# Hybrid decoder layer with hierarchical MoE, one core: TensorE's combination and gather spread between weight halves, parts of h and of the output made one pair later

## The chip, the cores and the metric

The kernel runs on one core of a Trainium2 chip. The metric is the device time of one execution in microseconds; three executions of the kernel before gave a median of 925.91 us (925.41 to 926.84).

## The reference

One decoder layer over 256 tokens of width 1024. First a mixing sub-layer: one projection of the normed input into a short gated convolution, a GLU with a 31-tap convolution and a cross-attention, merged by gates and projected again. Then the part that this case is about, the mixture of experts:

```python
g_sel = argmax(softmax(z @ w_group + b_group))          # 1 of 4 groups
top2  = top_k(softmax(e_logits of that group), 2)       # 2 of its 8 experts
for e in range(32):
    gate, up = split(z @ w_gate_up[e], 2)               # 1024 -> 2 x 512
    y += combine[:, e] * ((silu(gate) * up) @ w_down[e])   # 512 -> 1024
out = rms_norm(x + y, final_norm_g)
```

All arithmetic is float32 in the reference. The 32 experts' weights are 201 MB, and all of them are read.

## The kernel before

**Split weights.** TensorE multiplies with operands of the rounded type fp32r, so each float32 weight is used as a sum of two parts. A weight "half" is a tile of 128 x 2048 float32. It arrives in `raw` by DMA (two halves a transfer, six slots); ScalarE (ACT) makes the rounded part `hi` (`expert_hi`, L578), VectorE (DVE) makes `lo = raw - hi` (`expert_lo`, L932), and TensorE (PE) multiplies both. The `hi` and `lo` rings hold four halves (three and `hi_last`/`lo_last`): `expert_hi` of half N waits until TensorE has used half N-4. SyncE (SP) issues the next transfer into a raw slot once both `lo` parts of the slot are made (`lo_made`).

**Pairs.** Experts e and e+16 make a pair; there are 16 pairs, numbered i from 0. A pair has eight halves for gate and up and four for down. All experts' tokens of a pair are put into 2 x 64 slots by one-hot matmuls. A `step(j, r)` on each engine handles pair i = 2j + r: steps (0,0) and (0,1) are written out, the other 14 are in a hardware loop. Down halves of a pair are used in the next pair's step. In a step, halves have numbers k: 0 to 3 are gate (into PSUM bank G0), 4 to 7 up (G1), 8 to 11 the downs of pair i-1 (banks DN, the same two banks 6 and 7 that the gather writes). Halves 12 and 13 are halves 0 and 1 of the next step.

**The small work of a pair**, beside the halves:
- TensorE: `gather` (48 bf16 matmuls, L1305) picks the next pair's tokens out of `z_parts` into banks 6 and 7; `picked` (8 small ones, L1382 and L1387) makes the slots' weights and the transposed one-hot matrix in G0 and signals `slotted`; the fold matmuls (L1397, L1407) turn gate and up; `combine` (8 matmuls, L1341) adds the output of pair i-2 to the sums in banks 0 to 3.
- ScalarE: `gate_out` (`gu_sb`, L637) copies G0 out, `expert_xeT` (L484) makes the rounded part of the gathered tokens, `put` (L647) copies the transposed one-hot matrix out of G0, `up_out` (L654), `silu_sb` (L660), `hT_hi` (L616) rounds h, `y_out` (`y_hi`, L611) rounds the output in DN.
- VectorE: `xeT_lo` (L997), `slot_weights` (`fold2` L1048 and `comb_slot` L1051), `make_pick` (L1004), h = silu x up (L1083, `h_made`), `hT_lo` (L1041), `y_out_lo` (two instructions, L1055).

**Order.** Each engine runs its list in the order written, and semaphores join them. `put` waits for `comb_slot_made` as well as for `slotted`, since it and DVE's `slot_weights` read the same bank G0:

```python
expert_xeT(i + 1, (r + 1) % 2)
more(8)
act.wait_ge(comb_slot_made, i + 1)
act.wait_ge(slotted, i + 1)
nc.scalar.activation(put[:, r, :], G0[:, T:2 * T], ACT.Copy).then_inc(put_made, 1)
more(9)
```

`more(k)` is half k's `expert_hi` on ScalarE and `expert_lo` on VectorE. In the steps but the first the order of ScalarE is halves 2, 3, 4, 5, `gate_out`, 6, 7, `expert_xeT`, 8, `put`, 9, 10, `up_out`, 11, silu, 12, 13, `hT_hi`, `y_out`; that of VectorE is halves 2 to 7, `xeT_lo`, `slot_weights`, 8, 9, `make_pick`, 10, 11, 12, h, 13, `hT_lo`, `y_out_lo`; that of TensorE is halves 0, 1, `combine`, 2, 3, `gather`, 4, 5, `picked`, 6, 7, fold of gate, 8, 9, fold of up, 10, 11. In the first step there are no downs, and halves 0 to 3 are made ahead of it.

Of the kernel before, what the change touches and what calls it, by code (L numbers as in the profile page):

```python
# [23 lines left out]
KT = D // P  # L24
TT = T // P
# [13 lines left out]
STEP = 12  # L39
# [36 lines left out]
DENSE = 2 * N_UNITS  # L76
# [16 lines left out]
def hybrid_moe_kernel(nc, x, mem, w_dense, w_experts, w_route, cols, rows, consts, out):  # L93
    ctx = ExitStack()
    with ctx:
# [91 lines left out]
        hi_made, lo_made, half_used = sem("hi_made"), sem("lo_made"), sem("half_used")  # L187
# [35 lines left out]
        G0, G1 = ps[:, 4, :], ps[:, 5, :]  # L223
# [163 lines left out]
        def _(act):  # L387
# [93 lines left out]
            def expert_xeT(i, par):  # L481

                act.wait_ge(gathered, i + 1)
                nc.scalar.activation(xeT[:, par, :, :, 0:SLOTS], gathered_view(), ACT.Copy).then_inc(xeT_hi, 1)  # L484
# [120 lines left out]
            nc.scalar.activation(ident_bf[:, :], ident, ACT.Copy).then_inc(ident_made, 1)  # L605
            expert_xeT(0, 0)

            def y_out(i, used):

                act.wait_ge(half_used, used)  # L610
                nc.scalar.activation(y_hi[:, :], ps[:, 6:8, :].rearrange("p a b -> p (a b)"), ACT.Copy).then_inc(y_hi_made, 1)  # L611

            def hT_hi(i):

                act.wait_ge(h_made, i + 1)
                nc.scalar.activation(hT[:, :, :, 0:SLOTS], h_sb[:, :, :, :], ACT.Copy).then_inc(h_hi, 1)  # L616

            def step(j, r):


                start = isinstance(j, int) and j == 0 and r == 0
                i = 2 * j + r
                at_half = 0 if start else STEP * r - 4
                used = 2 * STEP * j + (DENSE + at_half)

                def more(*halves):
                    for k in halves:
                        expert_hi(j, at_half, k)

                if start:  # L630
                    more(4, 5)
                else:
                    more(2, 3, 4, 5)
                act.wait_ge(half_used, used + 4)
                if not start:
                    act.wait_ge(gate_folded, i)
                nc.scalar.activation(gu_sb[:, 0:FF], G0, ACT.Copy).then_inc(gate_out, 1)  # L637
                more(6, 7)
                if start:
                    act.wait_ge(comb_made, 1)  # L640
                    act.wait_ge(loops_made, 1)
                expert_xeT(i + 1, (r + 1) % 2)
                more(8)

                act.wait_ge(comb_slot_made, i + 1)
                act.wait_ge(slotted, i + 1)
                nc.scalar.activation(put[:, r, :], G0[:, T:2 * T], ACT.Copy).then_inc(put_made, 1)  # L647
                more(9)
                if not start:
                    more(10)  # L650
                act.wait_ge(half_used, used + 8)
                if not start:
                    act.wait_ge(up_folded, i)
                nc.scalar.activation(gu_sb[:, FF:2 * FF], G1, ACT.Copy, scale=comb_slot[:, r:r + 1]).then_inc(up_out, 1)  # L654
                if not start:
                    more(11)
                act.wait_ge(gate_folded, i + 1)
                if not start:
                    act.wait_ge(h_lo, i)
                nc.scalar.activation(silu_sb[:, :, :, :].rearrange("p f x s -> p (f x s)"), G0, ACT.Silu).then_inc(silu_made, 1)  # L660
                if not start:
                    more(12, 13)
                    act.wait_ge(half_used, used + 12)
                hT_hi(i)
                if not start:
                    y_out(i - 1, used + 12)

            step(0, 0)
            step(0, 1)
# [2 lines left out]
            with act.Fori(1, last_turn + 1) as j:  # L672
                step(j, 0)
                step(j, 1)
            expert_hi(last_turn, 2 * STEP - 4, 2)
            expert_hi(last_turn, 2 * STEP - 4, 3)
            act.wait_ge(half_used, 2 * STEP * last_turn + (DENSE + 2 * STEP))
# [15 lines left out]
        def _(dve):  # L693
# [340 lines left out]
                link(nc.vector.tensor_tensor(stat[:, 13:14], stat[:, 13:14], stat[:, 14:15], ALU.add))  # L1034
            nc.vector.tensor_scalar(loops[:, 0:1], stat[:, 13:14], float(TURNS - 1), None, ALU.add).then_inc(loops_made, 1)

            def hT_lo(i):

                dve.wait_ge(h_made, i + 1)
                dve.wait_ge(h_hi, i + 1)  # L1040
                nc.vector.tensor_tensor(hT[:, :, :, SLOTS:2 * SLOTS], h_sb[:, :, :, :], hT[:, :, :, 0:SLOTS].bitcast(f32),  # L1041
                                        ALU.subtract).then_inc(h_lo, 1)

# [14 lines left out]
            def step(j, r):  # L1058
                first = isinstance(j, int)
                i = 2 * j + r  # L1060
                start = first and i == 0
                at_half = 0 if start else STEP * r - 4

                def more(*halves):
                    for k in halves:
                        expert_lo(j, at_half, k)

                if start:
                    more(4, 5, 6, 7)
                else:  # L1070
                    more(2, 3, 4, 5, 6, 7)
                xeT_lo(i + 1, (r + 1) % 2)
                slot_weights(i, r)
                more(8, 9)
                make_pick(r, slice(r + 2, r + 3) if first else bass.ds(2 * j + (r + 2), 1))
                if not start:
                    more(10, 11, 12)
                dve.wait_ge(silu_made, i + 1)
                dve.wait_ge(up_folded, i + 1)
                if not start:  # L1080
                    dve.wait_ge(h_lo, i)
                up = G1[:, 0:4 * SLOTS].rearrange("p (f o s) -> p f o s", o=1, s=SLOTS).to_broadcast([P, 4, 2, SLOTS])
                nc.vector.tensor_tensor(h_sb[:, :, :, :], silu_sb[:, :, :, :], up, ALU.mult).then_inc(h_made, 1)  # L1083
                if not start:
                    more(13)
                hT_lo(i)
                if not start:
                    dve.wait_ge(y_hi_made, i)
                    for g in range(2):
                        y_out_lo(g, DN[g], y_lo_made)  # L1090

            step(0, 0)
            step(0, 1)
# [2 lines left out]
            with dve.Fori(1, last_turn + 1) as j:  # L1096
                step(j, 0)
                step(j, 1)
            expert_lo(last_turn, 2 * STEP - 4, 2)
            expert_lo(last_turn, 2 * STEP - 4, 3)  # L1100
            dve.wait_ge(half_used, 2 * STEP * last_turn + (DENSE + 2 * STEP))
            for g in range(2):
# [13 lines left out]
        def _(pe):  # L1116
# [176 lines left out]
            mm(ps[:, 5, 2 * PAIRS:3 * PAIRS], ones, either[:, 1, :], start=False, stop=True).then_inc(ranked, 1)  # L1293


            def gather(i, par):

                pe.wait_ge(pick_made, i + 1)
                for c in range(KT):
                    dst = ps[:, 6 + c // 4, c % 4 * 2 * SLOTS:(c % 4 + 1) * 2 * SLOTS]  # L1300
                    for k in range(3 * TT):
                        part_, t = k // TT, k % TT
                        if isinstance(i, int) and i == 0 and c == 0:
                            pe.wait_ge((z_part0, z_part1, z_part2)[part_], t + 1)
                        last = mm(dst, z_parts[:, part_, t, c * P:(c + 1) * P],  # L1305
                                  pick2[:, par, t, 0:2 * SLOTS],
                                  start=(k == 0), stop=(k == 3 * TT - 1))
                last.then_inc(gathered, 1)

            def gate_or_up(j, at_half, k, par):  # L1310

# [21 lines left out]
                                      stop=(x == 1 and h == 1 and kt == 1 and w is lo), skip_group_check=True)  # L1333
                last.then_inc(half_used, 1)

            def combine(par):

                for t in range(TT):
                    for g in range(2):
                        for y in (y_hi[:, g * 512:(g + 1) * 512], y_lo[g][:, :]):  # L1340
                            last = mm(Y[2 * t + g], put[:, par, t * P:(t + 1) * P], y,  # L1341
                                      start=False, stop=False, skip_group_check=True)
                    last.then_inc(combined, 1)
# [5 lines left out]
            def step(j, r, q):  # L1349
# [9 lines left out]
                if not first:  # L1359
                    pe.wait_ge(put_made, i - 1)  # L1360
                    pe.wait_ge(y_lo_made, 2 * i - 2)
                    combine(r)
                gate_or_up(j, at_half, 2, r)
                gate_or_up(j, at_half, 3, r)
                gather(i + 1, (r + 1) % 2)
                if not start:
                    pe.wait_ge(h_made, i)
                else:
                    pe.wait_ge(loops_made, 1)
                gate_or_up(j, at_half, 4, r)  # L1370
                gate_or_up(j, at_half, 5, r)

                pe.wait_ge(gate_out, i + 1)
                def picked(t, x):
# [42 lines left out]
            with pe.Fori(1, last_turn + 1) as j:  # L1417
                step(j, 0, bass.ds(j % TURNS * 2, 1))
                step(j, 1, bass.ds(j % TURNS * 2 + 1, 1))

            pe.wait_ge(put_made, 2 * last_turn + 1)
            pe.wait_ge(y_lo_made, 4 * last_turn + 2)
            combine(0)
            pe.wait_ge(silu_made, 2 * last_turn + 2)
            pe.wait_ge(h_made, 2 * last_turn + 2)
            pe.wait_ge(h_lo, 2 * last_turn + 2)
            for k in range(4):
                down(last_turn, 2 * STEP - 4, k, k // 2, (G0, G1))
            pe.wait_ge(put_made, 2 * last_turn + 2)
            pe.wait_ge(last_lo, 2)  # L1430
            combine(1)
# [54 lines left out]
```

## Time and profile before

| | |
|---|---|
| median of 3 executions | 925.91 us |
| the profiled execution's own time | 929.3 us |
| its span (first to last instruction) | 927.5 us |
| PE / DVE / ACT busy in the span | 873.3 / 814.4 / 621.7 us |
| expert stage, first to last h (L1083) | 432.3 to 898.9 us |

The profile is one execution. Its instructions have start times from the beginning of the span. A row of the timeline gives start, duration, engine, line, operation, tiles and count, and in brackets how long the engine sat idle before it and what ended that. An instruction's duration on ScalarE, VectorE and TensorE reaches a little beyond the start of the next one, since they are pipelined, so the time that an instruction takes from its engine's list is the distance between two starts.

### The profile page before, as it was taken

To read this page: it belongs to the slowest core of one execution; us is meant where nothing else is said; L and a number is where in the kernel's file an instruction comes from. 1 tells how busy PE (TensorE), PEld (TensorE's weight loads), DVE (VectorE), ACT (ScalarE), POOL (GpSimd) and SP (SyncE) were. 2 spreads that over 40 slices of the span, in tenths; PEclk is the share of its full clock that TensorE was granted. 3 is DMA by queue.
4 is the path that set the end of the run, shared out by engine and by line. 5 is a ranking of instruction groups with operands and counts; after the bars stand their busy time and mean duration, and the time that the engine had idled before them with its cause. 6 is when DMAs were issued, how large, how long until landed. Compare 5 with 4: busy or idle time off the path is not lost.

```text
span 927.5 us, 14508 instructions
## 1 busy us (share of the span) xinstructions
PE 873.3 (94%) x5734; PEld 751.2 (81%) x5734; DVE 814.4 (88%) x818; ACT 621.7 (67%) x537; POOL 11.0 (1%) x19
## 2 busy tenths in 40 slices
PE   5999999999999899868999999999999999999975
PEld 5999999999899899657877777777777877777764
DVE  5358999999867957488999999999999999999993
ACT  5563434345453573558888878888888878887882
POOL 0110000000000000020000000000000000000000
PEclk9999999999999999979999999999999999999997
DMA  9952545455443486518999999999999999999911
GB/s 379 374 183 97 210 155 194 170 184 194 159 155 119 182 317 267 211 37 327 384 400 399 411 395 407 398 411 400 401 408 408 396 400 406 409 398 396 423 66 45
DMA packets 20146, 270.64 MB, mean 292 GB/s; under 512 B 2192, under 2 KB 2448, under 8 KB 3856
## 3 DMA queue, kind: packets, MB, share of 16 engines
q1 hardware_dynamic: 19696, 268.59, 73.0%
q10 hardware_dynamic: 416, 1.57, 0.5%
q8 instruction: 24, 0.39, 0.2%
q14 instruction: 10, 0.08, 0.0%
HBM read 269.10 MB, written 1.05 MB: 291 GB/s over the span
## 4 chain that ended last, share of the span: by engine, by line
PE 48%; DVE 30%; issue 14%; ACT 6%; DMA 1%; DVEq 1%; SPq 0%; ACTq 0%
DVE lo L932 10%; PE ps L1317 10%; PE ps L1146 9%; PE ps L1147 9%; PE ps L1148 9%; DVE lo_last L932 7%; ACT hi L578 5%; PE ps L1305 3%; DVE lo L704 2%; DVE conv L791 2%; PE ps L1161 2%; PE ps L1163 2%; PE ps L1162 2%; DVE y_lo L1055 1%; DVE hT L1041 1%
## 5 line engine op out<-in xcount | busy, mean ns | idle before, releaser
L932 DVE TENSOR_TENSOR lo<-raw,hi 128x2048 fp32r<-128x2048 f32 x142 | 323.5, 2287 | 7.6 <-ACT hi L578 6.6
L578 ACT ACTIVATE hi<-raw 128x2048 fp32r<-128x2048 f32 x141 | 264.2, 1909 | 3.5 <-PE ps L1317 3.5
L1317 PE MATMUL ps<-hi,xeT 128*128 128x512 f32 x384 | 158.4, 412 | 15.1 <-DVE lo L932 11.2
L704 DVE TENSOR_TENSOR lo<-raw,hi 128x2048 fp32r<-128x2048 f32 x62 | 141.7, 2288 | 30.0 <-ACT hi L396 28.5
L1146 PE MATMUL ps<-inA,hi 128*128 128x256 f32 x576 | 165.1, 287 | 1.6 <-DVE lo L704 1.1
L1147 PE MATMUL ps<-inA,hi 128*128 128x256 f32 x576 | 163.8, 284 | 0.0
L1148 PE MATMUL ps<-inA,lo 128*128 128x256 f32 x576 | 163.7, 284 | 0.0
L396 ACT ACTIVATE hi<-raw 128x2048 fp32r<-128x2048 f32 x63 | 120.6, 1914 | 63.6 <-PE ps L1148 41.0
L1317 PE MATMUL ps<-lo,xeT 128*128 128x512 f32 x384 | 150.7, 392 | 0.0
L1146 PEld LDWEIGHTS ps<-inA,hi 128*128 128x128 f32 x576 | 111.4, 193 | 2.7 <-DVE lo L704 2.6
L1147 PEld LDWEIGHTS ps<-inA,hi 128*128 128x128 f32 x576 | 111.5, 194 | 0.1
L1148 PEld LDWEIGHTS ps<-inA,lo 128*128 128x128 f32 x576 | 111.4, 193 | 0.0
L1317 PEld LDWEIGHTS ps<-hi,xeT 128*128 128x128 f32 x384 | 72.1, 188 | 47.9 <-DVE lo L932 31.2
L932 DVE TENSOR_TENSOR lo_last<-raw,hi_last 128x2048 fp32r<-128x2048 f32 x48 | 109.7, 2285 | 0.0
L791 DVE SCALAR_TENSOR_TENSOR conv<-u_sb,col,conv 128x255 f32<-128x255 f32 (+29 forms) x240 | 94.1, 464 | 0.0
L578 ACT ACTIVATE hi_last<-raw 128x2048 fp32r<-128x2048 f32 x48 | 91.6, 1909 | 0.0
L1317 PEld LDWEIGHTS ps<-lo,xeT 128*128 128x128 f32 x384 | 72.2, 188 | 13.2
L1146 PE MATMUL ps<-inB,hi 128*128 128x256 f32 x256 | 72.7, 284 | 0.9 <-DVE lo L704 0.9
L1147 PE MATMUL ps<-inB,hi 128*128 128x256 f32 x256 | 72.4, 283 | 0.0
L1148 PE MATMUL ps<-inB,lo 128*128 128x256 f32 x256 | 72.4, 283 | 0.0
L1331 PE MATMUL ps<-hi,hT 128*128 128x512 f32 x192 | 63.9, 414 | 0.0
L1331 PE MATMUL ps<-lo,hT 128*128 128x512 f32 x192 | 60.2, 395 | 0.0
(214 smaller groups left out, 1229.5 us busy)
## 6 DMA issues: line engine op xcount, KB each, us to landing
raw<-in_w_experts SPq DMA_DIRECT2D x96, 2048.0 KB, 9.8
raw<-in_w_dense SPq DMA_DIRECT2D x29, 2048.0 KB, 7.8
raw<-in_w_dense SPq DMA_DIRECT2D x2, 1024.0 KB, 8.1
x_sb<-in_x SPq DMA_DIRECT2D x1, 1024.0 KB, 4.8
mem_sb<-in_mem SPq DMA_DIRECT2D x1, 1024.0 KB, 15.5
x_again<-in_x ACTq DMA_DIRECT2D x1, 1024.0 KB, 5.0
out<-x SPq DMA_DIRECT2D x2, 512.0 KB, 2.7
ffn_row<-in_rows ACTq DMA_DIRECT2D x1, 512.0 KB, 7.4
```

Source lines behind the costliest of these rows:

```text
L396: return nc.scalar.activation(conv_half(hi, N), raw_half(slot, h), ACT.Copy)
L578: nc.scalar.activation(expert_half(hi, N0), raw_flat(slot, k % 2), ACT.Copy).then_inc(hi_made, 1)
L704: nc.vector.tensor_tensor(conv_half(lo, N), raw_half(slot, h), conv_half(hi, N).bitcast(f32), ALU.subtract).then_inc(lo_made, 1)
L791: nc.vector.scalar_tensor_tensor(conv[:, c, shift:T], u_sb[:, c, 0:T - shift], w, conv[:, c, shift:T], ALU.mult, ALU.add).then_inc(conv_st ...
L932: nc.vector.tensor_tensor(expert_half(lo, N0), raw_flat(expert_slot(m), k % 2), expert_half(hi, N0).bitcast(f32), ALU.subtract).then_inc(l ...
L1146: mm(dst, w_hi[:, k, c * P:(c + 1) * P], acts[:, 0, k, :], start=(k == 0), stop=False)
L1147: mm(dst, w_hi[:, k, c * P:(c + 1) * P], acts[:, 1, k, :], start=False, stop=False)
L1148: last = mm(dst, w_lo[:, k, c * P:(c + 1) * P], acts[:, 0, k, :], start=False, stop=(k == KT - 1))
L1161: mm(dst, acts[:, 0, 4 * h + k, tok], w_hi[:, k, :], start=first, stop=False, skip_group_check=True)
L1305: last = mm(dst, z_parts[:, part_, t, c * P:(c + 1) * P], pick2[:, par, t, 0:2 * SLOTS], start=(k == 0), stop=(k == 3 * TT - 1))
L1317: last = mm(dst, xeT[:, par, 4 * (k % 2) + kt, k // 2 % 2, :], expert_half(w, N)[:, kt * 512:(kt + 1) * 512], start=(k % 4 == 0 and kt == ...
L1331: last = mm(DN[g], hT[:, 2 * h + kt, x, :], expert_half(w, N)[:, a:a + 512], start=(x == 0 and h == 0 and kt == 0 and w is hi), stop=(x == ...
```

## The change

The combination of pair i-2 is cut in two (token tile 0 before half 2, tile 1 before half 3) and the gather in three (three, three and two column tiles, after halves 3, 4 and 5; its start flags now stand once per bank). `hT_hi`, `hT_lo` and `y_out`, `y_out_lo` move from the end of a step into the next step. ScalarE makes half 6 before `gate_out`, and halves 7 and 8 after it; VectorE makes half 8 before `xeT_lo`. After the last step, the last pair's first three down halves go before `combine(0)`. The core of the diff (ScalarE, VectorE, TensorE in turn):

```diff
                 if start:
-                    more(4, 5)
+                    more(4, 5, 6)
                 else:
-                    more(2, 3, 4, 5)
+                    more(2)
+                    if not isinstance(j, int):
+                        y_out(used)
+                    more(3, 4)
+                    act.wait_ge(half_used, used)
+                    hT_hi(i)
+                    more(5, 6)
                 act.wait_ge(half_used, used + 4)
...
-                more(6, 7)
                 if start:
+                    more(7)
                     act.wait_ge(comb_made, 1)
                     act.wait_ge(loops_made, 1)
+                else:
+                    more(7, 8)
                 expert_xeT(i + 1, (r + 1) % 2)
-                more(8)
-
                 act.wait_ge(comb_slot_made, i + 1)
                 act.wait_ge(slotted, i + 1)
                 nc.scalar.activation(put[:, r, :], G0[:, T:2 * T], ACT.Copy).then_inc(put_made, 1)
+                if start:
+                    more(8)
                 more(9)
...
                 if not start:
                     more(12, 13)
-                    act.wait_ge(half_used, used + 12)
-                hT_hi(i)
-                if not start:
-                    y_out(i - 1, used + 12)
...
+            act.wait_ge(half_used, 2 * STEP * last_turn + (DENSE + 2 * STEP - 4))
+            hT_hi(2 * last_turn + 2)
+            y_out(2 * STEP * last_turn + (DENSE + 2 * STEP - 4))
             expert_hi(last_turn, 2 * STEP - 4, 2)
             expert_hi(last_turn, 2 * STEP - 4, 3)
```
```diff
-                    more(2, 3, 4, 5, 6, 7)
+                    more(2)
+                    if not first:
+                        dve.wait_ge(y_hi_made, i - 1)
+                        for g in range(2):
+                            y_out_lo(g, DN[g], y_lo_made)
+                    more(3, 4)
+                    hT_lo(i)
+                    more(5, 6, 7, 8)
                 xeT_lo(i + 1, (r + 1) % 2)
                 slot_weights(i, r)
-                more(8, 9)
+                if start:
+                    more(8)
+                more(9)
                 make_pick(r, slice(r + 2, r + 3) if first else bass.ds(2 * j + (r + 2), 1))
...
                     more(13)
-                hT_lo(i)
-                if not start:
-                    dve.wait_ge(y_hi_made, i)
-                    for g in range(2):
-                        y_out_lo(g, DN[g], y_lo_made)
...
+            hT_lo(2 * last_turn + 2)
             expert_lo(last_turn, 2 * STEP - 4, 2)
+            dve.wait_ge(y_hi_made, 2 * last_turn + 1)
+            for g in range(2):
+                y_out_lo(g, DN[g], y_lo_made)
             expert_lo(last_turn, 2 * STEP - 4, 3)
```
```diff
-                    combine(r)
+                    combine(r, (0,))
                 gate_or_up(j, at_half, 2, r)
+                if not first:
+                    combine(r, (1,))
                 gate_or_up(j, at_half, 3, r)
-                gather(i + 1, (r + 1) % 2)
+                gather(i + 1, (r + 1) % 2, (0, 1, 2))
...
                 gate_or_up(j, at_half, 4, r)
+                gather(i + 1, (r + 1) % 2, (3, 4, 5))
                 gate_or_up(j, at_half, 5, r)
+                gather(i + 1, (r + 1) % 2, (6, 7))
...
-            pe.wait_ge(put_made, 2 * last_turn + 1)
-            pe.wait_ge(y_lo_made, 4 * last_turn + 2)
-            combine(0)
             pe.wait_ge(silu_made, 2 * last_turn + 2)
             pe.wait_ge(h_made, 2 * last_turn + 2)
             pe.wait_ge(h_lo, 2 * last_turn + 2)
-            for k in range(4):
-                down(last_turn, 2 * STEP - 4, k, k // 2, (G0, G1))
+            down(last_turn, 2 * STEP - 4, 0, 0, (G0, G1))
+            down(last_turn, 2 * STEP - 4, 1, 0, (G0, G1))
+            down(last_turn, 2 * STEP - 4, 2, 1, (G0, G1))
+            pe.wait_ge(put_made, 2 * last_turn + 1)
+            pe.wait_ge(y_lo_made, 4 * last_turn + 2)
+            combine(0)
+            down(last_turn, 2 * STEP - 4, 3, 1, (G0, G1))
```

## Rows read from the trace of the kernel before

**Rows 1.** The page's slices of the granted TensorE clock, 40 over the span

```profile
PEclk9999999999999999979999999999999999999997
```

**Rows 2.** Busy time by stretch: one pair, and a stretch near the end

```profile
617.10:648.30 31.20, 30.32 (x177) 23.61 (x176) 30.89 (x21) 26.14 (x20) 0.00 (x0) 1.00 0.99 404
...
903.60:909.60 6.00, 5.96 (x14) 4.70 (x15) 4.39 (x2) 1.22 (x1) 0.00 (x0) 0.51 0.00 0
```

**Rows 3.** Waits from 500 to 900 us: total, times, longest

```profile
ACT put L647 <- DVE comb_slot L1051: 18.8, 13, 1.4
...
DVE lo L932 <- ACT hi L578: 3.5, 13, 0.3
```

**Rows 4.** Timeline of VectorE over one pair

```profile
618.15 0.68 DVE L1083 TENSOR_TENSOR silu_sb<-silu_sb,ps 128x512 f32<-128x512 f32 x1
...
620.95 0.68 DVE L1041 TENSOR_TENSOR hT<-silu_sb,hT 128x512 fp32r<-128x512 f32 x1
621.55 1.28 DVE L1055 TENSOR_TENSOR y_lo<-ps,y_hi 128x512 fp32r<-128x512 f32 x2
...
627.15 4.49 DVE L932 TENSOR_TENSOR lo<-raw,hi 128x2048 fp32r<-128x2048 f32 x2
631.89 2.29 DVE L932 TENSOR_TENSOR lo<-raw,hi 128x2048 fp32r<-128x2048 f32 x1 [0.25 <-ACT hi L578]
...
636.30 1.22 DVE L997 TENSOR_TENSOR xeT<-ps,xeT 128x1024 fp32r<-128x1024 f32 x1
...
637.63 0.16 DVE L1051 TENSOR_REDUCE comb_slot<-ps 128x1 f32<-128x6 f32 x1
637.71 4.63 DVE L932 TENSOR_TENSOR lo<-raw,hi 128x2048 fp32r<-128x2048 f32 x2
...
649.33 0.68 DVE L1083 TENSOR_TENSOR silu_sb<-silu_sb,ps 128x512 f32<-128x512 f32 x1
```

**Rows 5.** Timeline of ScalarE in the same pair

```profile
629.46 0.60 ACT L637 ACTIVATE gu_sb<-ps 128x512 f32<-128x512 f32 x1 [1.78 <-PE ps L1317]
...
633.57 1.01 ACT L484 ACTIVATE xeT<-ps 128x1024 fp32r<-128x1024 f32 x1
...
637.82 0.39 ACT L647 ACTIVATE put<-ps 128x256 fp32r<-128x256 f32 x1 [1.44 <-DVE comb_slot L1051]
638.11 3.71 ACT L578 ACTIVATE hi<-raw 128x2048 fp32r<-128x2048 f32 x2
```

**Rows 6.** Timeline of TensorE: a gather and the first matmuls of the half behind it

```profile
598.00 2.85 PE L1305 MATMUL ps<-pick,z_parts 128*128 128x128 bf16 x48
...
600.66 0.48 PE L1317 MATMUL ps<-hi,xeT 128*128 128x512 f32 x1
...
600.98 0.39 PE L1317 MATMUL ps<-lo,xeT 128*128 128x512 f32 x1
```

**Rows 7.** Timeline of the first pair, all engines

```profile
418.88 2.85 PE L1305 MATMUL ps<-pick,z_parts 128*128 128x128 bf16 x48
...
425.91 1.22 DVE L997 TENSOR_TENSOR xeT<-ps,xeT 128x1024 fp32r<-128x1024 f32 x1
...
427.32 4.63 DVE L932 TENSOR_TENSOR lo<-raw,hi 128x2048 fp32r<-128x2048 f32 x2
...
430.26 1.28 ACT L660 ACT_TABLE_LOAD   x1
```

**Rows 8.** Timeline behind the last h, VectorE and then TensorE

```profile
898.90 0.68 DVE L1083 TENSOR_TENSOR silu_sb<-silu_sb,ps 128x512 f32<-128x512 f32 x1
...
901.70 0.69 DVE L1041 TENSOR_TENSOR hT<-silu_sb,hT 128x512 fp32r<-128x512 f32 x1
...
903.64 0.80 PE L1341 MATMUL ps<-y_hi,put 128*128 128x512 f32 x1 [4.66 <-DVE y_lo L1055]
...
915.11 0.61 PE L1331 MATMUL ps<-lo_last,hT 128*128 128x512 f32 x2
```

**Rows 9.** The expert transfers' time from issue to landing, 560 to 700 us

```profile
DMA to landing us min/median/max: 9.1/9.7/10.9
```

More of the change, by code:

```diff
@@ L606, in _, with y_out, hT_hi @@
             expert_xeT(0, 0)
-            def y_out(i, used):
+            def y_out(used):
                 act.wait_ge(half_used, used)
                 nc.scalar.activation(y_hi[:, :], ps[:, 6:8, :].rearrange("p a b -> p (a b)"), ACT.Copy).then_inc(y_hi_made, 1)
-            def hT_hi(i):
-                act.wait_ge(h_made, i + 1)
+            def hT_hi(count):
+                act.wait_ge(h_made, count)
                 nc.scalar.activation(hT[:, :, :, 0:SLOTS], h_sb[:, :, :, :], ACT.Copy).then_inc(h_hi, 1)
@@ L1035, in _, with hT_lo @@
             nc.vector.tensor_scalar(loops[:, 0:1], stat[:, 13:14], float(TURNS - 1), None, ALU.add).then_inc(loops_made, 1)
-            def hT_lo(i):
-                dve.wait_ge(h_made, i + 1)
-                dve.wait_ge(h_hi, i + 1)
+            def hT_lo(count):
+                dve.wait_ge(h_made, count)
+                dve.wait_ge(h_hi, count)
                 nc.vector.tensor_tensor(hT[:, :, :, SLOTS:2 * SLOTS], h_sb[:, :, :, :], hT[:, :, :, 0:SLOTS].bitcast(f32),
@@ L1293, in _, with gather @@
             mm(ps[:, 5, 2 * PAIRS:3 * PAIRS], ones, either[:, 1, :], start=False, stop=True).then_inc(ranked, 1)
-            def gather(i, par):
+            def gather(i, par, tiles=range(KT)):
                 pe.wait_ge(pick_made, i + 1)
-                for c in range(KT):
+                for c in tiles:
                     dst = ps[:, 6 + c // 4, c % 4 * 2 * SLOTS:(c % 4 + 1) * 2 * SLOTS]
@@ L1306, in gather @@
                                   pick2[:, par, t, 0:2 * SLOTS],
-                                  start=(k == 0), stop=(k == 3 * TT - 1))
-                last.then_inc(gathered, 1)
+                                  start=(k == 0 and c % 4 == 0), stop=(k == 3 * TT - 1), skip_group_check=True)
+                if c == KT - 1:
+                    last.then_inc(gathered, 1)
             def gate_or_up(j, at_half, k, par):
@@ L1334, in down, with combine @@
                 last.then_inc(half_used, 1)
-            def combine(par):
-                for t in range(TT):
+            def combine(par, tiles=range(TT)):
+                for t in tiles:
                     for g in range(2):
@@ L1419, in _ @@
                 step(j, 1, bass.ds(j % TURNS * 2 + 1, 1))
+            pe.wait_ge(silu_made, 2 * last_turn + 2)
+            pe.wait_ge(h_made, 2 * last_turn + 2)
+            pe.wait_ge(h_lo, 2 * last_turn + 2)
+            down(last_turn, 2 * STEP - 4, 0, 0, (G0, G1))
+            down(last_turn, 2 * STEP - 4, 1, 0, (G0, G1))
+            down(last_turn, 2 * STEP - 4, 2, 1, (G0, G1))
             pe.wait_ge(put_made, 2 * last_turn + 1)
@@ L1423, in _ @@
             combine(0)
-            pe.wait_ge(silu_made, 2 * last_turn + 2)
-            pe.wait_ge(h_made, 2 * last_turn + 2)
-            pe.wait_ge(h_lo, 2 * last_turn + 2)
-            for k in range(4):
-                down(last_turn, 2 * STEP - 4, k, k // 2, (G0, G1))
+            down(last_turn, 2 * STEP - 4, 3, 1, (G0, G1))
             pe.wait_ge(put_made, 2 * last_turn + 2)
```

## The prediction

> **What bounds the kernel now.** I read the busy time by stretch first, then the waits of the expert stage, then the timeline of one pair engine by engine; the whole-span shares say little, since the change touches only the expert stage. In the stretch of one pair VectorE is busy 30.89 of 31.20 us, TensorE 30.32, and ScalarE 26.14 [rows 2]. TensorE's share flatters it: a matmul's bar overlaps the next one's. Counted by starts, a half of eight matmuls takes 0.32 us for the first and 0.23 for each other one, 1.93 us; the 48 matmuls of a gather take 2.66 us (598.00 to 600.66) [rows 6]. Twelve halves are 23.2 us, the gather 2.7, the eight matmuls of the combination 1.9: 27.8 us, with some 2 us of small matmuls beside them, so TensorE has between one and two us to spare in a pair. VectorE has none. Two starts of h, 618.15 and 649.33, are 31.18 us apart, and between them the reader finds only two holes in VectorE's list [rows 4]. One is before half 6: halves 4 and 5 start at 627.15, each takes 2.20 us from the list (4.49 less 2.29), so half 6 could start at 631.55; it starts at 631.89, 0.34 us late, and the row says that it waited for ScalarE's `hi`. The waits list the same hole 13 times from 500 to 900 us, 3.5 us in all (it counts from the end of the earlier bar, so each time a little less than the true delay) [rows 3]. ScalarE was late because `gate_out` stands ahead of half 6 and had waited 1.78 us for TensorE [rows 5]. The other hole is inside the two halves that start at 637.71: their common bar is 4.63 us and not 4.49, so half 9 starts at 640.05 (637.71 + 4.63 - 2.29), 0.14 us late.
>
> So VectorE's own list, 31.18 - 0.34 - 0.14 = 30.70 us a pair, is what a change of order can reach at best, and what counts is every place where VectorE waits. Transfers don't count: they land 9.7 us after their issue [rows 9], a slot's turn is 31 us (six slots, six transfers a pair), and no `hi` waits for one. They are issued when `lo` parts are made, so they follow VectorE's pace.
>
> **The change part by part, in a pair of the loop.** VectorE's instructions are the same ones in another order, so its list stays 30.70 us; what changes are its waits.
>
> *Half 6 ahead of `gate_out`.* The hole of 0.34 us goes. The new `hi` of half 6 no longer waits for `gate_out`, but for half 2 on TensorE, since the ring holds four halves. Counted from the start of h: VectorE is through with h, half 13, half 2 and y_lo at 0.60 + 2 x 2.20 + 1.20 = 6.2; TensorE then has four combination matmuls (0.93) and half 2 (1.93), to about 9.2, and ScalarE's `hi` (1.91) is ready at about 11.2. VectorE wants it at 6.2 + 3 x 2.20 + 0.60 = 13.4, behind halves 3, 4, hT_lo and 5. So 2 us are to spare. Gain 0.34.
>
> *`hT` and `y` one step later.* Their price on VectorE is unchanged: 0.60 for hT_lo (620.95 to 621.55) and twice 0.60 for y_lo [rows 4]. On ScalarE the y_hi now stands ahead of halves 3 and 4, but it is made while VectorE does halves 13 and 2, and ScalarE is idle 5 us in a pair [rows 2]. The downs that need hT come at half 8, five halves behind the place where hT_lo is now made. Zero.
>
> *The combination.* TensorE waits at its first part for the second y_lo. Behind it in TensorE's queue stand halves 2 to 5, the gather and `slotted`. Count from the moment VectorE's list is through with y_lo: TensorE can start about 0.12 us later, and needs 1.86 for the eight combination matmuls, 4 x 1.93 for halves 2 to 5 and 2.66 for the gather, 12.3 in all with the 0.12. The last gather matmul ends 0.17 later; `expert_xeT` starts 0.12 after that and takes 1.01 [rows 5]: 13.6 to 13.7 us. VectorE gets to `xeT_lo` after halves 3, 4, hT_lo, 5, 6, 7, 8: 6 x 2.20 + 0.60 = 13.8 us. So the gathered tokens are just in time, by 0.1 to 0.2 us. This is the tightest place. Splitting the gather puts two more changes between bf16 and fp32 matmuls into the queue; rows 6 show the change at 0.09 us (0.32 against 0.23, which each half pays anyway). Between nothing and 0.6 us late a pair are the ends; I take nothing, the nearer to the row.
>
> *`put` ahead of half 9, with half 8 moved away.* This is the large one. `put` waits for `comb_slot`, which VectorE makes; half 9's `hi` stands behind `put` on ScalarE. Before, VectorE went from `comb_slot` to half 8, whose `hi` was long made, and that 2.20 us hid the path: `comb_slot` at 637.63 to 637.79, `put` at 637.82, `hi` of half 9 at 638.11, its `lo` at 640.05 [rows 4, 5]. Only 0.14 us stuck out. Now half 8 is already behind VectorE when it makes `comb_slot`, and the next thing in its list is half 9. Nothing else is there to do. The path is the same, so VectorE stands from the start that was 637.71 to 640.05: 2.34 us, in every pair. It can't be less: `hi` of half 9 can't start before `put`, nor `put` before `comb_slot`. Cover gone, the whole `put` + `hi` shows.
>
> Sum of a pair: 30.70 + 2.34 = 33.04 us against 31.18: 1.86 us more. There are 14 such pairs between the second h and the last: +26.0.
>
> **The first two steps.** In step 0 VectorE's half 8 and ScalarE's half 8 both stay behind `slot_weights`, but `put` now comes before half 8. The gather also ends later. From 418.88, where the old gather started [rows 7]: 18 matmuls 1.00, half 4 1.91, 18 more 1.00, half 5 1.91, 12 more 0.67, then 0.17 + 0.12 + 1.01 + 0.04 to `xeT_lo`: 426.71 instead of 425.91. `comb_slot` is through 1.41 us later (425.91 to 427.32 in the row), at 428.12, and half 8 starts 2.34 later at 430.46; half 9 follows at once at 432.66, where it started at 429.66 (427.32 + 4.63 - 2.29). So the first h is 3.0 us later. From there to the second h VectorE has one half and the y_lo fewer than in a full pair: 30.70 - 2.20 - 1.20 + 2.34 = 29.64 us, and about 0.5 more because ScalarE, with its 1.28 us table load [rows 7], gets to half 10 only at about 436.4 while VectorE is free at 435.9. Before, the first interval was 898.90 - 432.34 - 14 x 31.18 = 30.0 (432.34 is 427.32 with two halves, 0.14 and the pick behind it). So +0.1. Together the last h comes 3.0 + 0.1 + 26.0 = 29.1 us later.
>
> **The end.** Before, TensorE started its last 40 matmuls of this part (combination and four downs) at 903.64, 4.74 us behind the last h, because y_lo had to come first [rows 8]. Now it starts with the downs once hT_lo is made: h 0.60, half 2.20, hT_lo 0.69, 0.04: 3.53 us. The y_lo and the two last halves are ready while the first three downs run (y_lo about 6.9 us behind h, the downs busy until 9 or later). That is 1.2 us saved. The 40 matmuls took until about 915.6, 12 us against the 9.3 that full clock would give, at a granted clock of 0.51 from 903.6 to 909.6 [rows 2], that is 1.2 GHz of 2.4, after an idle time of 4.66. The new idle time is 3.5 us; whether the clock still falls no row shows. Ends: 0 and 2.7 us saved. I take 0, the value of the only row.
>
> **Sum.** 29.1 - 1.2 = +27.9 us. On the profiled execution's 929.3 us that is 957.2; the timed runs' median lies 3.4 us under it, so I predict 925.91 + 27.9 = 953.8.
>
> **The rivals.**
>
> *The gathered tokens come late.* My 0.2 us of slack rests on spacings added over 88 matmuls. If they are 0.5 us worse, VectorE waits 0.3 to 0.4 more in each of 14 pairs, +5: 959. For: the chain is long, with three gather pieces. Against: spacings are regular in every row. It would add to the stall, not replace it. 13%.
>
> *TensorE's clock falls in the loop.* TensorE's work is the same and a pair is 1.86 us longer, so it idles that much more, with the longest gap of about 1.5 us before the combination (half 1 ends 4.8 us behind h's start, y_lo at 6.3). Now every slice of the expert stage has full clock [rows 1], with waits at nearly every half; the one fall in rows 2 came after 4.66 us. If a dip came in each pair and cost what the end's did, 2.7 us, less the 0.2 of slack, it would be 14 x 2.5 = 35 us more, 989. 2%. The Trainium skill's page "TensorE: Matmul & The Clock Gate" says under "A second HAM failure mode: psum-queue depth-cycling" that small idle times between matmul groups, if frequent enough, make the clock swing between its two levels. By that rule the clock would already fall here, in a stage with a wait at nearly every half; rows 1 and 2 show it at 1.00, so I give it little.
>
> *The other side: faster.* The hole before half 6 goes, and `put` costs VectorE nothing, because half 9's `hi` is there when `comb_slot` is through. Then a pair takes 30.70 us, 0.48 less, and the whole 15 x 0.48 + 1.2 = 8.4 us less: 917.5. What speaks for it is that `gate_out`'s hole is real and is removed. It decides by the order on ScalarE alone: if `hi` 9 came before `put`; by the diff it comes behind, so this needs an error of reading. The point of balance is a stall of 0.5 us where I count 2.34. 3%; and 1% that gain and stall cancel within 0.2%, which is about what a measurement can tell from no change here (1.9 us).
>
> **How the numbers follow.** Forecast 81%, tokens late 13%, clock 2%, faster 3%, no change 1%. The range takes the end's 2.7 us on the low side with some for the first steps, and the late tokens on the high side: 948 to 960. Slower by over 0.2%: 0.96; within: 0.01; faster: 0.03.
>
> **What would show it.** Distance between starts of h: 33.0 us. In VectorE's timeline an idle of about 2.3 us in front of one `lo` a pair, behind `comb_slot`, released by ScalarE's `hi`, and no idle in front of half 6. VectorE's share of a pair's stretch about 0.93. TensorE's idle before the last downs 3.5 us. It is wrong if that idle is under 0.5 us, if `xeT_lo` waits by more than 0.3 us, or if the granted clock in the loop is under 1.00.

## The result and the profile after

The changed kernel took 953.15 us (median of four executions, 952.81 to 954.79) against 926.38 for the kernel before: ratio 1.0292, 95% interval 1.0274 to 1.031. It is slower by 26.8 us; the prediction said 953.8.

Busy time by stretch of the changed kernel, one pair from one h to the next (stretch and length, then TensorE, its weight loads, VectorE, ScalarE and GpSimd, granted clock, DMA share, GB/s); it answers to [rows 2]:

```profile
593.77:626.81 33.04, 30.20 (x177) 23.59 (x176) 30.79 (x22) 26.38 (x20) 0.00 (x0) 1.00 0.97 381
```

VectorE is busy for 30.8 us, as before (30.9), but the pair is 33.04 us long, a share of 0.93. TensorE, ScalarE and the transfers do what they did; the granted clock is full. So the lost time is idle time of VectorE. Its waits from 500 to 900 us (total, times, longest), to compare with [rows 3]:

```profile
...
DVE lo L939 <- ACT hi L578: 27.0, 12, 2.3
ACT put L653 <- DVE comb_slot L1058: 22.5, 12, 1.9
...
ACT gu_sb L643 <- PE ps L1333: 9.6, 12, 0.8
```

The wait of `lo` on `hi` was 3.5 us in 13 pairs and is now 27.0 in 12, 2.25 each. VectorE's timeline of that pair, to be laid beside [rows 4]:

```profile
593.77 0.68 DVE L1099 TENSOR_TENSOR silu_sb<-silu_sb,ps 128x512 f32<-128x512 f32 x1
594.37 4.49 DVE L939 TENSOR_TENSOR lo<-raw,hi 128x2048 fp32r<-128x2048 f32 x2
598.77 1.29 DVE L1062 TENSOR_TENSOR y_lo<-ps,y_hi 128x512 fp32r<-128x512 f32 x2
...
604.37 0.69 DVE L1048 TENSOR_TENSOR hT<-silu_sb,hT 128x512 fp32r<-128x512 f32 x1
604.97 4.49 DVE L939 TENSOR_TENSOR lo<-raw,hi 128x2048 fp32r<-128x2048 f32 x2
609.37 2.29 DVE L939 TENSOR_TENSOR lo_last<-raw,hi_last 128x2048 fp32r<-128x2048 f32 x1
611.58 2.29 DVE L939 TENSOR_TENSOR lo<-raw,hi 128x2048 fp32r<-128x2048 f32 x1
613.78 1.23 DVE L1004 TENSOR_TENSOR xeT<-ps,xeT 128x1024 fp32r<-128x1024 f32 x1
614.91 0.29 DVE L1055 TENSOR_TENSOR fold<-cst,ps 128x128 f32<-128x128 f32 x1
615.11 0.17 DVE L1058 TENSOR_REDUCE comb_slot<-ps 128x1 f32<-128x6 f32 x1
617.52 2.29 DVE L939 TENSOR_TENSOR lo<-raw,hi 128x2048 fp32r<-128x2048 f32 x1 [2.25 <-ACT hi L578]
...
626.81 0.68 DVE L1099 TENSOR_TENSOR silu_sb<-silu_sb,ps 128x512 f32<-128x512 f32 x1
```

The reader finds one bracket in the whole pair. Half 6 (609.37) has none: that hole is gone. Half 9 could start at 615.18 and starts at 617.52. ScalarE shows why; it answers to [rows 5]:

```profile
612.39 1.03 ACT L484 ACTIVATE xeT<-ps 128x1024 fp32r<-128x1024 f32 x1 [1.67 <-PE ps L1320]
615.30 0.39 ACT L653 ACTIVATE put<-ps 128x256 fp32r<-128x256 f32 x1 [1.89 <-DVE comb_slot L1058]
615.59 3.71 ACT L578 ACTIVATE hi<-raw 128x2048 fp32r<-128x2048 f32 x2
```

`put` starts 0.02 us behind `comb_slot`'s end, the `hi` of half 9 behind `put`, and `lo` 0.03 behind `hi` (the first of the two, of 1.90). Both engines stand in turn: ScalarE 1.89 us for VectorE's `comb_slot`, then VectorE 2.25 for ScalarE's `hi`.

The first step on VectorE (compare [rows 7]), with one idle time before the tokens, one behind `comb_slot` and a short one behind h, before the first half whose `hi` stands behind ScalarE's table load:

```profile
422.76 1.23 DVE L1004 TENSOR_TENSOR xeT<-ps,xeT 128x1024 fp32r<-128x1024 f32 x1 [2.19 <-ACT xeT L484]
...
426.50 4.49 DVE L939 TENSOR_TENSOR lo<-raw,hi 128x2048 fp32r<-128x2048 f32 x2 [2.25 <-ACT hi L578]
...
431.38 0.68 DVE L1099 TENSOR_TENSOR silu_sb<-silu_sb,ps 128x512 f32<-128x512 f32 x1
432.59 2.29 DVE L939 TENSOR_TENSOR lo<-raw,hi 128x2048 fp32r<-128x2048 f32 x1 [0.52 <-ACT hi L578]
```

The end, VectorE and then TensorE (compare [rows 8]):

```profile
924.12 0.68 DVE L1099 TENSOR_TENSOR silu_sb<-silu_sb,ps 128x512 f32<-128x512 f32 x1
...
926.92 0.69 DVE L1048 TENSOR_TENSOR hT<-silu_sb,hT 128x512 fp32r<-128x512 f32 x1
...
927.84 0.73 PE L1347 MATMUL ps<-hi,hT 128*128 128x512 f32 x2 [3.68 <-DVE hT L1048]
```

and its stretches there, the granted clock third from the right; it is low in the one and nearly full in the next, where [rows 2] have 0.51 over six us:

```profile
928.00:932.00 4.00, 4.00 (x12) 3.09 (x13) 3.79 (x4) 1.98 (x2) 0.00 (x0) 0.59 0.00 0
932.00:936.00 4.00, 4.00 (x19) 3.32 (x18) 1.90 (x1) 0.00 (x0) 0.00 (x0) 0.98 0.00 0
```

### The profile page after: what moved, and what is told of

It is laid out like the page before. It is cut to its first block, busy times and chain, and to the rows that moved or that the text cites. A ratio compares the mean times of both kernels' runs of the same rounds, so it can differ in the third digit from the quotient of the medians.

```text
span 951.0 us, 14519 instructions
## 1 busy us (share of the span) xinstructions
PE 868.9 (91%) x5734; PEld 747.8 (79%) x5734; DVE 813.1 (86%) x818; ACT 625.3 (66%) x537; POOL 11.0 (1%) x19
## 4 chain that ended last, share of the span: by engine, by line
DVE 38%; PE 36%; issue 20%; ACT 5%; DMA 1%; DVEq 1%; ACTq 0%; SPq 0%
DVE lo L939 16%; PE ps L1161 9%; PE ps L1163 8%; PE ps L1162 8%; DVE lo_last L939 7%; ACT hi L578 3%; DVE xeT L1004 2%; DVE lo L711 2%; DVE conv L798 2%; PE ps L1176 1%; PE ps L1178 1%; PE ps L1177 1%; DVE y_lo L1062 1%; PE ps L1333 1%; DVE silu_sb L1099 1%
## 5 line engine op out<-in xcount | busy, mean ns | idle before, releaser
L1161 PEld LDWEIGHTS ps<-inA,hi 128*128 128x128 f32 x576 | 109.8, 191 | 2.6 <-DVE lo L711 2.5
L1162 PEld LDWEIGHTS ps<-inA,hi 128*128 128x128 f32 x576 | 109.8, 191 | 0.1
```

The costliest lines, as they stand in the source:

```text
L1161: mm(dst, w_hi[:, k, c * P:(c + 1) * P], acts[:, 0, k, :], start=(k == 0), stop=False)
L1162: mm(dst, w_hi[:, k, c * P:(c + 1) * P], acts[:, 1, k, :], start=False, stop=False)
```

## The experiments

The table is read from VectorE's timelines of all kernels: from the first `xeT_lo` (start of the expert stage) to the first h, from there to the second, the mean distance of the 14 that follow, and the time from the last h to VectorE's last instruction. All in us, with the median and its ratio to the kernel before on the same chip.

| kernel | to first h | to second | mean of 14 | end | median | ratio, 95% interval |
|---|---|---|---|---|---|---|
| before | 22.14 | 29.74 | 31.20 | 25.47 | 926.4 | 1 |
| changed | 25.14 | 30.25 | 33.035 | 23.72 | 953.2 | 1.0274 to 1.031 |
| e1: put behind half 9 | 25.14 | 27.90 | 30.78 | 23.36 | 919.2 | 0.9911 to 0.9959 |
| e2: VectorE's half 8 back | 25.14 | 29.23 | 32.73 | 24.41 | 950.2 | 1.0237 to 1.0273 |
| e3: before, VectorE's half 8 early | 22.13 | 32.07 | 33.51 | 25.55 | 961.6 | 1.0362 to 1.0397 |
| e4: before, half 6 first | 21.97 | 29.44 | 30.84 | 25.21 | 921.3 | 0.9928 to 0.9966 |
| e5: half 8 back, gather whole | 21.96 | 28.66 | 30.84 | 24.46 | 919.5 | 0.9905 to 0.995 |
| e6: half 8 back, gather in pieces | 23.24 | 29.04 | 32.98 | 24.30 | 950.2 | 1.022 to 1.0269 |
| e7: before, half 6 first, put behind 9 | 21.97 | 29.29 | 30.69 | 25.41 | 918.3 | 0.9899 to 0.9929 |
| e9: changed, end undone | 25.15 | 30.24 | 33.03 | 25.33 | 956.1 | 1.0301 to 1.0336 |
| e10: changed, gather whole behind half 5 | 22.85 | 28.32 | 30.69 | 23.34 | 917.8 | 0.9889 to 0.9922 |
| e11: changed, once more | 25.16 | 30.25 | 33.03 | 23.78 | 953.5 | 1.0269 to 1.0316 |
| e12: e9's kernel, once more | 25.14 | 30.25 | 33.03 | 25.05 | 954.9 | 1.0284 to 1.0328 |

**e1, the stall taken away.** In the changed kernel, ScalarE's list in all steps but the first:

```diff
                 expert_xeT(i + 1, (r + 1) % 2)
+                if not start:
+                    more(9)
                 act.wait_ge(comb_slot_made, i + 1)
...
                 if start:
-                    more(8)
-                more(9)
-                if not start:
+                    more(8, 9)
+                else:
                     more(10)
```

> The changed kernel with one thing moved: in every step but the first, ScalarE makes half 9 ahead of put instead of behind it. Theory (the stall is put + hi of half 9, 2.34 us a pair behind comb_slot): the hi of half 9 is then ready about when VectorE gets there, a hole of 0.2 us is left, distance of two h 33.03 -> 30.9 us, total 953.2 - 14 x 2.1 - 2.3 = about 921. Rival (TensorE's cut-up combination and gather, or the two extra y and hT waits, cost the time): VectorE still has idle before xeT_lo or y_lo, distance stays at or above 32.5 us, total over 945.

Measured 919.16 us, 30.78 a pair. One `more(9)` moved over one copy takes 34 us off: 31.5 in the 14 pairs, 2.35 in the interval ahead of them. The kernel is now faster than the one before, by 0.7%. In the first step, which this edit leaves alone, the stall stays (25.14 to the first h, as in the changed kernel). ScalarE, and then VectorE, of e1:

```profile
602.58 1.91 ACT L578 ACTIVATE hi<-raw 128x2048 fp32r<-128x2048 f32 x1
604.57 0.38 ACT L655 ACTIVATE put<-ps 128x256 fp32r<-128x256 f32 x1
```
```profile
604.37 0.17 DVE L1059 TENSOR_REDUCE comb_slot<-ps 128x1 f32<-128x6 f32 x1
604.52 2.29 DVE L940 TENSOR_TENSOR lo<-raw,hi 128x2048 fp32r<-128x2048 f32 x1
```

`hi` of half 9 ends at 604.49 and `lo` starts at 604.52, 0.07 us behind the earliest start; I had reckoned 0.2. `put` still starts at `comb_slot`'s end, since until then ScalarE was idle.

**e3, the stall made in the kernel before.** Only VectorE's list is changed (and again not in the first step):

```diff
-                    more(2, 3, 4, 5, 6, 7)
+                    more(2, 3, 4, 5, 6, 7, 8)
                 xeT_lo(i + 1, (r + 1) % 2)
                 slot_weights(i, r)
-                more(8, 9)
+                if start:
+                    more(8)
+                more(9)
```

> The kernel before with a single move: VectorE's half 8 ahead of xeT_lo in all steps but the first. Nothing of TensorE, hT or y is changed. Theory: the stall of 2.34 us behind comb_slot appears here too, and the old hole of 0.34 us before half 6 stays: distance of two h 31.18 + 2.2 to 2.35 = 33.4 to 33.5 us, total 926.4 + 15 x 2.25 = about 960. Rival (the cost comes from TensorE's new order): no change, 926.

Measured 961.60 us, 33.51 a pair. VectorE of e3 has both holes, the old one before half 6 and the new one behind `comb_slot`:

```profile
610.31 2.29 DVE L932 TENSOR_TENSOR lo<-raw,hi 128x2048 fp32r<-128x2048 f32 x1 [0.31 <-ACT hi L578]
...
618.37 0.16 DVE L1051 TENSOR_REDUCE comb_slot<-ps 128x1 f32<-128x6 f32 x1
620.78 2.29 DVE L932 TENSOR_TENSOR lo<-raw,hi 128x2048 fp32r<-128x2048 f32 x1 [2.25 <-ACT hi L578]
```

With TensorE's order, hT and y as they were, the whole loss is there, and more of it than in the changed kernel. e1 and e3 together settle the cause from both sides.

**e2, VectorE's half 8 back.** In the changed kernel `more(5, 6, 7, 8)` becomes `more(5, 6, 7)`, and `more(8, 9)` stands behind `slot_weights`.

> The changed kernel with VectorE's half 8 put back behind slot_weights (ScalarE as in the change). Theory: put is covered again, but VectorE now reaches xeT_lo 2.20 us earlier than before, and the gathered tokens, late by the gather spread over halves 4 and 5, are not there: an idle of about 2.0 us moves to the front of xeT_lo, and 0.15 is left before half 9; distance of two h 32.8 us, total 949 to 950. Rival (only the place of half 8 against put costs time, the gather's spread is free): distance 30.8 us, total about 920.

Measured 950.20 us, 32.73 a pair. The stall changes its place:

```profile
613.32 1.23 DVE L1004 TENSOR_TENSOR xeT<-ps,xeT 128x1024 fp32r<-128x1024 f32 x1 [1.83 <-ACT xeT L484]
...
614.66 0.16 DVE L1058 TENSOR_REDUCE comb_slot<-ps 128x1 f32<-128x6 f32 x1
614.73 4.63 DVE L939 TENSOR_TENSOR lo<-raw,hi 128x2048 fp32r<-128x2048 f32 x2
```

`put` is covered as in [rows 4] (a bar of 4.63), but now the tokens are late by 1.9 us. So the gather in pieces does need half 8 ahead of `xeT_lo`, and half 8 there uncovers `put`. Each of the two edits is paid for by the other.

**e5 and e6, with half 8 back on both engines**, and the gather whole behind half 3 (e5) or in its three pieces (e6). The common edit on ScalarE:

```diff
                 else:
-                    more(7, 8)
+                    more(7)
                 expert_xeT(i + 1, (r + 1) % 2)
+                more(8)
                 act.wait_ge(comb_slot_made, i + 1)
...
-                if start:
-                    more(8)
                 more(9)
```

> The changed kernel with two parts undone: half 8 back behind xeT_lo and slot_weights (VectorE) and behind expert_xeT, ahead of put (ScalarE), and the gather whole again behind half 3. Left of the change: half 6 first, the cut combination, hT and y one step later, the end. Theory: with half 8 back put is covered and with the gather whole the tokens are early: no large wait, holes of 0.13 and 0.16 us at fold2 and half 9, distance of two h 30.9 to 31.0 us, total 920. Rival (the later hT and y, or the cut combination, cost something of their own): over 925.

> The changed kernel with half 8 back behind xeT on both engines (VectorE behind slot_weights, ScalarE between expert_xeT and put), but the gather still in three pieces. It differs from the run with the gather whole by the gather alone. Theory: the tokens come after half 5, while VectorE reaches xeT_lo one half earlier than in the change: idle of about 1.8 to 2.0 us before xeT_lo and 0.4 before half 8 (its hi stands behind expert_xeT), distance of two h 33.0 us, total 951 to 953. Rival (the spread gather is free wherever it ends): as with the gather whole, 30.84 us and 919.5.

e5: 919.51 us, 30.84 a pair, a little under the range given, since the expected hole at `fold2` isn't there in the loop. e4 below, which has neither the cut combination nor the later hT and y, has 30.84 too, so these cost nothing measurable. e6: 950.17 us, 32.98 a pair (the total 1 us under the range given, the distance as expected). VectorE of e6:

```profile
614.40 1.22 DVE L1003 TENSOR_TENSOR xeT<-ps,xeT 128x1024 fp32r<-128x1024 f32 x1 [1.79 <-ACT xeT L484]
...
616.20 4.49 DVE L938 TENSOR_TENSOR lo<-raw,hi 128x2048 fp32r<-128x2048 f32 x2 [0.31 <-ACT hi L578]
```

**e4, half 6 alone**, in the kernel before: `more(2, 3, 4, 5, 6)` ahead of `gate_out` and `more(7)` behind it (`more(4, 5, 6)` in the first step).

> The kernel before with a single move: ScalarE's half 6 ahead of gate_out in all steps. Theory: the hole of 0.34 us before half 6 goes in each of 15 intervals (the new hi waits only for half 2 on TensorE), and 0.9 us in the first step; distance of two h 31.18 -> 30.85, total 926.4 - 14 x 0.34 - 1.3 = about 920.3. Rival (the hole only moves, since another wait ends right behind it): under 2 us gained.

Measured 921.29 us. The pairs gain 0.36 us each, as expected. The first step gains 0.17 and not 0.9. Its ScalarE and VectorE show where the rest went:

```profile
427.59 0.69 ACT L654 ACTIVATE gu_sb<-ps,comb_slot 128x512 f32<-128x512 f32 x1 [1.13 <-PE ps L1317]
```
```profile
428.70 0.55 DVE L1004 TENSOR_TENSOR pick<-cst,rank_tab 128x384 bf16<-128x384 f32 x1
430.21 0.69 DVE L1083 TENSOR_TENSOR silu_sb<-silu_sb,ps 128x512 f32<-128x512 f32 x1 [0.96 <-ACT silu_sb L660]
```

h now waits for silu. Silu stands behind the table load of [rows 7], and that behind `up_out`, which waits for TensorE: it starts 19.35 us behind the first `xeT_lo` here (408.24) and in the kernel before (429.55 less 410.20) alike. So TensorE's halves, and behind them `up_out`, the table load and silu, hold the first h, and VectorE's gain turned into a new wait, which I had left out of this expectation.

**e7, both small holes of the kernel before removed** on ScalarE: e4's edit, and `more(8, 9)` ahead of `put`.

> The kernel before with two moves on ScalarE alone: half 6 ahead of gate_out, half 9 ahead of put. Theory: both holes in VectorE's list (0.34 and 0.14 us) go, distance of two h 30.68 to 30.70 us, 0.14 us less a pair than with half 6 alone: total 917.5 to 919. Rival (put later makes the fold of gate late on TensorE, and with it h): 921 or more.

Measured 918.29 us, 30.69 a pair: VectorE's own list, 30.70, with nothing left between.

**e10, the change with its stall mended otherwise.** The gather whole behind half 5, `more(7, 8, 9)` ahead of `expert_xeT`:

```diff
                 gate_or_up(j, at_half, 3, r)
-                gather(i + 1, (r + 1) % 2, (0, 1, 2))
...
                 gate_or_up(j, at_half, 4, r)
-                gather(i + 1, (r + 1) % 2, (3, 4, 5))
                 gate_or_up(j, at_half, 5, r)
-                gather(i + 1, (r + 1) % 2, (6, 7))
+                gather(i + 1, (r + 1) % 2)
```

> The changed kernel with three moves: ScalarE's half 9 ahead of expert_xeT and put (half 8 in the first step), VectorE's half 8 ahead of xeT_lo in the first step too, and TensorE's whole gather behind half 5 instead of in three pieces. Theory: TensorE's queue up to the last gather matmul holds the same work, so the tokens come at the same time, while halves 4 and 5 are used earlier and the hi of halves 8 and 9 are early: VectorE has no hole at all, distance of two h 30.68 to 30.70 us, the end as in the change: total 953.15 - 14 x 2.34 - 4.5 = about 915.9. Rival (tokens late by the gather's place): idle in front of xeT_lo, total over 919.

VectorE of e10 has no bracket in a pair of the loop; around `comb_slot`:

```profile
604.08 1.22 DVE L1003 TENSOR_TENSOR xeT<-ps,xeT 128x1024 fp32r<-128x1024 f32 x1
...
605.41 0.16 DVE L1057 TENSOR_REDUCE comb_slot<-ps 128x1 f32<-128x6 f32 x1
605.49 2.28 DVE L938 TENSOR_TENSOR lo<-raw,hi 128x2048 fp32r<-128x2048 f32 x1
```

Measured 917.78 us, the fastest of all, though its interval overlaps e7's. From the first `xeT_lo` to the last h it is 480.8 us (22.85 + 28.32 + 14 x 30.69), as expected (517.9 - 14 x 2.34 - 4.5 = 480.6); the total is 1.9 us above the expected one. Much of that can be the start of the expert stage: in e10's profiled execution (919.25 us) it starts at 410.14 us and in the changed kernel's (952.81 us) at 406.24, 3.9 us earlier, in code that the edit doesn't touch. For the other executions, which have no trace, it stays open. "No hole at all" was also wrong for the first step: there `more(9)` still stands behind `put` while half 8 has moved ahead, and VectorE waits 2.25 us (22.85 to the first h, against 21.96 in e5).

**e9, e11, e12, the end.** e9 is the changed kernel with its end undone: `combine(0)` ahead of the downs on TensorE, and on VectorE

```diff
-            expert_lo(last_turn, 2 * STEP - 4, 2)
             dve.wait_ge(y_hi_made, 2 * last_turn + 1)
             for g in range(2):
                 y_out_lo(g, DN[g], y_lo_made)
+            expert_lo(last_turn, 2 * STEP - 4, 2)
```

> The changed kernel with the end undone: combine(0) ahead of the last pair's downs on TensorE, and y_lo ahead of the next to last half on VectorE. Theory: TensorE then starts its last 40 matmuls about 1.1 us later (4.8 instead of 3.7 us behind the last h), total 954.2 against 953.15; distance of two h 33.03 as in the changed kernel. Rival (the end's order gained by the clock, not by the start): 2.5 us or more later, with a lower granted clock for longer.

It took 956.14 us, 3.0 above the changed kernel's median, but the two had not been run side by side. So e11 (the changed kernel) and e12 (e9's kernel) were run together:

> The changed kernel once more, for a comparison of its end with the undone end on the same chip. Theory: the new end is worth the earlier start of TensorE's last 40 matmuls, 1.0 us, and up to 0.6 by the clock: it is 1.0 to 1.7 us faster than the one with the end undone. Rival (the end's order is worth 3 us, as the two medians from different sessions suggest): 2.5 us or more faster.

> The changed kernel with the end undone (combine(0) ahead of the last pair's downs on TensorE, y_lo ahead of the next to last half on VectorE), on the same chip as the changed kernel. Theory: 1.0 to 1.7 us slower than it, distance of two h 33.03 in both. Rival: 2.5 us or more slower.

953.47 against 954.94 us: 1.5 us for the end. The executions' spreads (952.7 to 956.15 and 954.8 to 958.08) overlap, so the size is from one comparison; the profiles agree with it, 23.78 against 25.05 us from the last h (and 25.33 in e9). So about half of the 3.0 us was not the kernel's. TensorE of e9, where y_lo sets the start 4.74 us behind the last h (at 924.23), as in [rows 8]:

```profile
928.97 0.65 PE L1357 MATMUL ps<-y_hi,put 128*128 128x512 f32 x1 [4.66 <-DVE y_lo L1062]
```

## Why the prediction was right, step by step

- *The stall behind `comb_slot`*, 2.34 us by the prediction: 615.18 to 617.52 is 2.34. Taken away in e1 and made anew in e3.
- *The hole before half 6*: gone in the changed kernel, 0.36 us a pair when removed alone (e4), predicted 0.34.
- *The pair*: 33.04 predicted, 33.035 measured over 14. The old pair is 31.20 in the mean and not 31.18, so the 14 pairs add 25.7 us and not 26.0.
- *The gathered tokens* were to be in time by 0.1 to 0.2 us. `expert_xeT` ends at 613.42 and VectorE is free for it at 613.78, so some 0.3 us. The rival "tokens late" did not come true in the change, but e2 and e6 show that it is real once half 8 goes back: 1.8 us of idle time. In the first step they come 0.81 us later than before, counted from the first `xeT_lo` (16.52 against 15.71); 0.80 was predicted.
- *Combination, hT, y*: zero predicted; e5, which keeps them, stands at 30.84, and so does e4 without them.
- *The first two steps*: the first h later by 25.14 - 22.14 = 3.00, as predicted. The interval behind it grew by 30.25 - 29.74 = 0.5, not 0.1: I had taken the old one as a remainder, 30.0, and it was 29.7. As a remainder of the same sum it made up for the error in the pairs, so the two cancel by their making and not by luck. The 0.5 us for ScalarE's table load is there as the wait of 0.52 at 432.59.
- *The last h*, counted from the first `xeT_lo`: 517.88 against 488.70, 29.2 later; predicted 29.1.
- *The end*: TensorE's last work starts 3.72 us behind the last h and not 4.74, so 1.0 saved and not 1.2 (its idle time is 3.68, predicted 3.5): the first matmul starts 0.23 us behind hT_lo's end, where I had put 0.04. The clock still fell, but for less of the work: from that start to ScalarE's next `y_hi` it is 11.0 us (927.84 to 938.85) and was 12.1 (903.64 to 915.76). Some 0.4 us of this 1.1 is lost again behind it, where the last three of eight combination matmuls run slowly, at a clock of 0.70 and then 0.50 from 942 us. In all the end is 25.47 - 23.72 = 1.75 us shorter. That lies between the prediction's two ends, nearer to the value that it took (1.2 and 3.9). e11 and e12 give 1.5.
- *The sum* by the profiles is 29.2 - 1.75 = 27.4 us; predicted 27.9, by the medians 26.8. That the total came within 0.7 us is in part luck: the difference was 1.1 us too large, and the median that it was added to, 925.91, came out 0.5 higher with a fourth execution.
- *The clock in the loop*: 1.00 in the pair's row and from 480 us to the last h, though TensorE waits 1.3 us for y_lo in each pair:

```profile
633.14 0.50 PE L1357 MATMUL ps<-y_hi,put 128*128 128x512 f32 x1 [1.29 <-DVE y_lo L1062]
```

  The Trainium skill's page "TensorE: Matmul & The Clock Gate", section "A second HAM failure mode: psum-queue depth-cycling", has a kernel whose clock swung on small gaps that came often. In this loop it didn't swing, with gaps of 1.3 us.

- *The clock in the first step*, ahead of the loop, did fall, and the prediction has no such term. TensorE waited 2.38 us for ScalarE's `up_out`, ran eight small matmuls and stood another 0.85 us:

```profile
428.90 1.10 PE L1427 MATMUL ps<-cst,gu_sb 128*128 128x64 f32 x8 [2.38 <-ACT gu_sb L662]
```
```profile
431.00:433.00 2.00, 2.00 (x5) 1.61 (x6) 1.48 (x3) 2.00 (x2) 0.00 (x0) 0.50 0.72 131
```

  e1, e9, e11 and e12 show the same fall. In the kernel before `up_out` comes in time, only the 0.85 us is there, and the clock stays at 1.00. No wait of VectorE up to the second h is for TensorE (they are 0.52 and 2.25 us, both for ScalarE's `hi`), so no cost of it is to be seen.

The two profiled executions alone would have misled: their spans differ by 951.0 - 927.5 = 23.5 us, since the expert stage started 3.96 us earlier in the changed kernel's (406.24 against 410.20), in code that the change doesn't touch. The forecast of a difference had to be made from one profile and added to the median.

## What to carry to other kernels

When one engine's list is the bound, look for every instruction pair of the form "A makes a small thing, B's small copy waits for it, and B's next large piece stands behind the copy": the path costs nothing only as long as A has a large piece of its own ready in between. Moving that piece ahead, to cover something else, uncovers the path. Before moving work on two engines, write both lists side by side and check, at each cross wait, what each side does while the other is at it; here one line moved over a copy was worth 34 us.

## What the runs showed that was not expected

The start of the expert stage, in code common to all kernels, falls into a few places: first `xeT_lo` at 406.2 to 406.9 us (changed, e1, e9, e11), 407.5 (e7), 408.2 to 408.4 (e2, e3, e4, e5) and 410.1 to 410.5 (before, e6, e10, e12). Between the profiles of before and of the changed kernel, 1.8 us of the 4.0 is there at the fourth half (`lo`) already, and stays to the end of the dense stage; the other 2.2 come behind 380 us, where the granted clock of the stretch from 380 to 390 us was 0.83 in the one and 1.00 in the other:

```profile
380.00:390.00 10.00, 8.28 (x42) 6.36 (x41) 3.91 (x5) 5.44 (x16) 0.00 (x0) 0.83 0.56 202
```
```profile
380.00:390.00 10.00, 9.09 (x53) 6.74 (x52) 5.97 (x8) 6.06 (x13) 0.00 (x0) 1.00 0.57 211
```

All thirteen traces fit these two differences, and they come independently. The fourth half starts at 23.2 to 24.0 us (changed, e1, e2, e3, e5, e7, e9, e11) or at 25.1 to 25.4 (before, e4, e6, e10, e12), and the clock from 380 to 390 us is 1.00 (changed, e1, e4, e7, e9, e11) or 0.83 (the others). From the fourth half to the start of the expert stage it is 382.8 to 383.5 us with the one and 384.9 to 385.2 with the other. So the same code differs by up to 4 us between executions: some 2 us go with the start, and some 2 with the clock. What decides either was not tried.
